# A hybrid decoder layer on one core: the weight sums of each block's first slot are formed one block earlier, in another buffer

## The reference, cut to what matters

```
hn   = rms_norm(x)
proj = hn @ w_in + b_in                      # q, k, v, o, gates, conv B, C, x
y_m  = sigmoid(o) * mlstm_chunkwise(q, k, v, gates)
y_c  = conv_b * causal_conv3(conv_c * conv_x)
x    = x + concat(y_m, y_c) @ w_out          # the output projection
hn2  = rms_norm(x)
x    = x + sum over 2 chosen of 32 experts of w * (silu(hn2 @ Wg) * (hn2 @ Wu)) @ Wd
out  = rms_norm(x)
```

## Time and profile before

| | us |
|---|---|
| median of 3 runs | 2068.16 (2067.43 to 2068.41) |
| the profiled execution | 2067.49 |
| its span, from first to last instruction | 2065.7 |
| PE busy | 1986.2 (96%) |
| DVE busy | 741.6 (36%) |
| POOL busy | 556.4 (27%) |
| ACT busy | 324.5 (16%) |

### The profile page before, as it was taken

The page is one execution under the profiler, slowest core; times in us unless marked ns, Lnnn a source line. Parts: engine busy times, 40 slices in busy tenths (PEclk is TensorE's granted clock), DMA queues, the critical chain, the costliest instruction groups (busy, mean ns, idle before and its releaser), DMA issues.

```text
span 2065.7 us, 29853 instructions
## 1 busy us (share of the span) xinstructions
PE 1986.2 (96%) x11060; PEld 1593.5 (77%) x11060; DVE 741.6 (36%) x1752; ACT 324.5 (16%) x756; POOL 556.4 (27%) x593
## 2 busy tenths in 40 slices
PE   6999999999999999999999699999999999999996
PEld 5888658888578885688875588888888888888884
DVE  3165435554353653346541422222222222222222
ACT  1011110111100211102111012221121112221120
POOL 5123021131040330212310133333333333333332
PEclk9999999999999999999999699999999999999998
DMA  3521412122312125121112688888988888888983
GB/s 146 211 80 64 173 72 83 64 80 107 138 64 80 62 79 186 62 79 66 62 51 93 232 305 318 319 329 322 339 331 328 318 320 320 319 323 333 344 320 119
DMA packets 76274, 394.56 MB, mean 191 GB/s; under 512 B 10579, under 2 KB 10836, under 8 KB 44320
## 3 DMA queue, kind: packets, MB, share of 16 engines
q1 hardware_dynamic: 45456, 291.43, 38.6%
q0 software_dynamic: 25984, 85.28, 10.7%
q10 hardware_dynamic: 4752, 16.80, 2.0%
HBM read 333.38 MB, written 60.10 MB: 190 GB/s over the span
## 4 chain that ended last, share of the span: by engine, by line
PE 93%; DVE 2%; issue 2%; POOL 1%; ACT 1%; DMA 0%; DVEq 0%; POOLq 0%; ACTq 0%
PE ps_proj L461 23%; PE ps_proj L630 11%; PE ps_proj L473 9%; PE ps_proj L682 7%; PE ps_proj L684 7%; PE ps_state L702 5%; PE ps_num L702 5%; PE ps_scores L684 3%; PE ps_rows L684 3%; PE ps_scores L682 3%; PE ps_rows L682 3%; PE ps_num L707 3%; PE ps_num L665 1%; PE ps_state L500 1%; PE ps_rows L588 1%
## 5 line engine op out<-in xcount | busy, mean ns | idle before, releaser
L473 PE MATMUL ps_proj<-ww,hnT 128*128 128x256 f32 (+1 forms) x1024 | 226.8, 382 | 4.4 <-DVE vx L1423 4.3
L682 PE MATMUL ps_proj<-hnT,wo 128*128 128x160 f32 x1024 | 226.9, 303 | 0.7 <-ACT hnT L845 0.7
L630 PE MATMUL ps_proj<-wo,yT 128*128 128x512 f32 x512 | 224.1, 593 | 0.0
L684 PE MATMUL ps_proj<-hnT,wo 128*128 128x160 f32 x1024 | 223.5, 300 | 0.0
L473 PEld LDWEIGHTS ps_proj<-ww,hnT 128*128 128x128 f32 x1024 | 193.3, 190 | 35.6 <-DVE vx L1423 7.3
L630 PEld LDWEIGHTS ps_proj<-wo,yT 128*128 128x128 f32 x512 | 96.0, 190 | 112.6 <-issue 112.4
L682 PEld LDWEIGHTS ps_proj<-hnT,wo 128*128 128x128 f32 x1024 | 166.7, 191 | 13.9 <-issue 13.9
L684 PEld LDWEIGHTS ps_proj<-hnT,wo 128*128 128x128 f32 x1024 | 167.7, 191 | 0.0
L461 PE MATMUL ps_proj<-hnT,ww 128*128 128x256 f32 x640 | 154.6, 385 | 1.4 <-DVE hnT L1146 1.0
L461 PEld LDWEIGHTS ps_proj<-hnT,ww 128*128 128x128 f32 x640 | 120.0, 192 | 20.3 <-issue 2.5
L1706 DVE TENSOR_TENSOR kT<-qT,ps_proj 128x160 f32<-128x160 f32 x64 | 17.7, 317 | 297.0 <-ACT qT L857 297.0
(11 more groups left out here) (307 smaller groups left out, 3157.0 us busy)
## 6 DMA issues: line engine op xcount, KB each, us to landing
wo<-in_w_gu SPq DMA_DIRECT2D x128, 1024.0 KB, 7.2
ww<-in_w_slots SPq DMA_DIRECT2D x52, 1024.0 KB, 4.9
og<-in_w_dn SPq DMA_DIRECT2D x32, 1024.0 KB, 5.6
vx<-in_w_dn SPq DMA_DIRECT2D x32, 1024.0 KB, 8.6
xin<-in_x SPq DMA_DIRECT2D x16, 512.0 KB, 5.0
hnT<-in_xT SPq DMA_DIRECT2D x8, 1024.0 KB, 9.0
xres<-in_x SPq DMA_DIRECT2D x16, 512.0 KB, 3.5
hn_rows<-hn ACTq DMA_DIRECT2D x16, 512.0 KB, 2.7
```

The lines of the kernel that those rows point to most:

```text
L473: mm = pe.matmul(PROJ[:, n % 2, 0:w], hnT[:, k, t * P:(t + 1) * P], slot_weights(slot, k, 0, w), start=(k == 0), stop=(k == KT - 1))
L630: mm = pe.matmul(PROJ[:, n % 2, :], yT[:, k, t * P:(t + 1) * P], wo[:, k, half * 512:(half + 1) * 512], start=(k == 0), stop=(k == KT - 1))
L682: pe.matmul(GU[m][:, 0:CAP], wo[:, kt, m * P:(m + 1) * P], xT[:, kt, :], start=(kt == 0), stop=(kt == KT - 1), skip_group_check=True)
L684: mm = pe.matmul(GU[m][:, CAP:2 * CAP], wo[:, kt, FF + m * P:FF + (m + 1) * P], xT[:, kt, :], start=False, stop=(kt == KT - 1), skip_group ...
```

## The change

The sums of slot 0 get a set of buffers of their own in `og`. For the first block they are formed ahead of POOL's loop. For block b + 1 they are formed in block b, ahead of `norm_scales(b + 1)`; they wait for slot 0 of block b + 1 in `ww[0]` and for `yn_ready` of block b's last chunk (the last reader of `og`), and no more for the end of the output projection. The sums of slot 1 stay where they were, in `yT` behind the projection.

```
+        oflat = og[:].rearrange("p t c -> p (t c)")
+        wsums.append([oflat[:, i * KH * P:(i + 1) * KH * P] for i in range(4)])
...
-            return wsums[s % 2 if s < RUN else 2 + s % 2][i - 1].rearrange("p (k c) -> p k c", c=P)
+            at = 4 if s == 0 else s % 2 if s < RUN else 2 + s % 2
+            return wsums[at][i - 1].rearrange("p (k c) -> p k c", c=P)
...
-                if s in (0, 1):
+                if s == 0:
+                    if not isinstance(b, int):
+                        pool.wait_ge(S_("yn_ready"), b * CT)
+                elif s == 1:
                     pool.wait_ge(S_("proj_done"), b * NU)
...
+            weight_sums(0, 0)
             with pool.Fori(0, NB) as b:
-                for s in range(RUN):
+                for s in range(1, RUN):
                     weight_sums(b, s)
...
                 with pool.If(b < NB - 1):
+                    weight_sums(b + 1, 0)
                     norm_scales(b + 1)
```

## The result

The changed kernel took 2046.97 us (median) against 2068.28 us for the kernel before on the same chip. The ratio is 0.9901, with a 95% interval of 0.9888 to 0.9914. The profiled execution took 2045.8 us with a span of 2044.1; the one before took 2067.49 with 2065.7.

The account below looks back on a forecast made before the run. PE was taken as the bound, stalled at block boundaries for POOL's second sum. 2067.5 - 19.6 + 1.2 = 2049.1 us for the profiled execution; with 0.7 for the median, 2049.8, range 2046.5 to 2056 (8 in 10).

Parts of the forecast that it names:

- Stall and slow stretch: At three block boundaries, PE's idle wait for POOL's second sum plus low-clock work behind it: 19.6 us saved, 11.8 idle.
- Why the sums were late: At a boundary, POOL could not write yT before the projection ended and reached the first sum at 294.84 us.
- Nothing takes the stall's place: After part 1 at the boundaries, input sums and slot 1's sums are ready before PE needs them; no new wait.
- The moved sums are free on POOL: At their new place, after slot 0 lands, POOL would otherwise be idle, 29.98 us before norm_scales; no POOL time lost.
- The collision: POOL's moved sums slow DVE's second pair of convolution taps; PE waits 0.4 us per boundary before round 35, +1.2 us total.
- rival 2: At the boundaries only the idle time comes back, as the clock falls for another reason: 2057.6 us; chance 7%.
- rival 3: At the boundaries slot 0's sums are early, but another wait ends at the same time: 2068 us; chance 4%.
- rival 4: On POOL the moved sums hold up norm_scales if slot 0 lands late: slower, 2077 us for 3 us past; chance 4%.
- rival 1: Beside the taps the shared-port collision costs its upper bound, 6.5 us in place of 1.2: 2055.1 us; chance 10%.
- nothing changes in the first block: The first block forms its sums from the same load at the same point, only into og: no difference in time.

Follow-up runs that it names:

- a0: The changed kernel again, unaltered, as the base on the second chip: 2045.63 us, against 2064.96 for the kernel before there.
- e3: The changed kernel with the block's last two calls exchanged, the moved sums behind norm_scales(b + 1): 2045.79 us.
- e5: The changed kernel with four more POOL additions of 128 x 512 between yn_ready and the moved sums: 2055.21 us.
- f0: The changed kernel again, unaltered, as the base on the third chip: 2045.0 to 2047.9 us in four runs.

## Why the prediction was right

The forecast was 2049.8 us in a range of 2046.5 to 2056; it came to 2047.0, inside, at the lower end. The mechanism was right from the stall on. That the number fell inside the range is partly luck: of the runs near 2046 us the median is 2045.8, 0.7 us below the range, and on the second chip it is 2045.63. The narrower range that the prediction gave its own forecast, 2048 to 2052, was missed, and the gain was forecast some 3 us too small.

- *Stall and slow stretch, 19.6 us*: measured 6.10 + 6.59 + 6.94 = 19.63. The filled stall shows that the slow stretch belongs to the stall.
- *Why the sums were late*: half right. The prediction put it down to the end of the projection, before which POOL could not write to `yT`. With the buffer alone, which lifts that wait, POOL still came at 294.54: what held it was its place behind the last small scale. The change moved both, so the error cost nothing.
- *Nothing takes the stall's place*: right. Part 6 started at 293.52 in the new profile, 1.81 us behind part 1; at the boundaries the third and fourth input sum and slot 1's sums are waited for nowhere.
- *The moved sums are free on POOL*: right; they start at 493.17 in block 1, 0.2 us or so behind the landing, and `norm_scales` did not move against ACT's squares.
- *The collision, +1.2 us*: right mechanism, size too high for the first profile (0.1 us in two blocks, none in block 0), but of the right size in others (0.74, 0.90 us in one block). Two L1510 lost 1.77 us, as the row had it (1.81); the L1507 ahead of them lost nothing, since DVE came to it first. The rule of the Trainium skill ("SBUF — State Buffer"), that whichever engine is first holds the shared ports for its whole instruction, would have cost 2.2 us a block if POOL had been first each time. No row of the changed kernel shows that: where POOL came ahead of the first tap (third chip, block 1), L1515 lost 0.94 us, the pair behind it 1.81, and PE waited 0.90. This does not speak against the rule, only against POOL being first at every operation. The kernel with twice the operations shows 2.55 us on PE, of which 1.62 before round 35.
- *Rivals*: rival 2 (only the idle time comes back) fell by the clock at 1.00 and by the filled stall; rival 3 by the boundaries of 6.99 us; rival 4 by the 11.46 us of idle time ahead of `norm_scales`; rival 1 (2.2 us a block) by waits before round 35 of 0.10 us in the first profile and of 0.90 us at most in the others of the changed kernel.

What was missing are 0.88 us at the start, where I wrote that nothing changes in the first block, and two differences that are not the change's: 0.86 us between the last boundary and the second expert, and 0.5 us from there to the end. For 0.5 us of the 0.86, PE at the router's table, before and after:

```profile
1151.68 4.53 PE L515 MATMUL ps_rows<-x,qw 128*64 128x160 f32 x16 [4.24 <-DVEq L1321]
```

```profile
1131.41 4.01 PE L518 MATMUL ps_rows<-x,qw 128*64 128x160 f32 x16 [4.24 <-DVEq L1329]
```

The same 16 instructions take 4.53 and 4.01 us behind a wait of 4.24 us each. The third chip's profile of the changed kernel has 4.53 there, so this belongs to the execution and not to the change. The same holds for the stretch behind the blocks as a whole, from PE's last group of the output projection (1121.25 before, 1100.98 after) to the end of the span: it takes 944.5 us in the profile before and 943.1 in the one after, but 944.1 in the changed kernel's on the third chip, and 942.7 to 944.8 over all twelve profiles. So 1.4 us of the missing 3.3 are the luck of the profiled execution. Together with the 0.88 and the 1.0 us by which the collision was overestimated they make the 3.3 us between the sum for the profiled execution (2049.1) and its 2045.8.

## What to carry to other kernels

A stall of the matrix engine costs its idle time and the slow stretch behind it; count from the work before the stall to a mark well behind it, not by the idle column. When a helper engine's work is late because of where it stands in its queue, look for a buffer that is free earlier, and check that buffer and place moved together: the buffer alone did nothing here. Where the work moves, look at what the vector engine does there with two inputs in SBUF; here each GpSimd operation beside such a tap cost it about 0.9 us, free only up to the slack of the next reader. And before a difference of 1 us is explained, look how much a stretch that the edit does not touch moves from one execution to the next: here 2 us.

## What the runs showed of the hardware

The kernels with the stall scatter more than those without. On the second chip the kernel before took 2058.8 to 2067.7 us in 15 runs and the one with the buffer alone 2061.5 to 2067.5 in 11, while the changed kernel took 2044.8 to 2046.8 in 4 (fewer runs, so its spread is known less well). With the stall filled it was 2058.9 to 2061.4, beside 2063.5 to 2068.7 for the kernel before. The mean granted clock goes with it: on the third chip the kernel before had 0.986 and 0.985 in its runs of 2062.6 and 2062.8 us, and 0.981 to 0.983 in those of 2066.7 to 2068.8. The 24 instructions behind the first boundary's stall took 6.94 us until the transposes in one profile and 7.57 in another (298.48 to 306.05 with the buffer alone), and 7.80 and 8.16 behind the other two stalls of the first profile, where 5.18 is full speed. Behind the wait at the very start it varies too: there the 24 instructions took 6.90 to 8.23 us until the next part in the five profiles with the changed kernel's order there (the first one, a0, e3, e5 and f0). So the return of the clock comes at a varying time after work starts again, and the gain of a removed stall is not one number: its fixed part is the idle time of 11.8 us, and the rest, 7.8 in the profile that I had, would be less against a lucky run: the fastest run of the kernel before on the second chip, 2058.75 us, lies only 13.1 us above the changed kernel's median.
